# A hybrid attention layer on one core: a new opening, a row-wise end, and a forget chain laid around a softmax

## What is computed

```
n = rmsnorm(h); u = n @ w_in   # q, k, v of mixers A and B, 8 forget logits, 2 gates
A: chunk-band attention, 8 heads x 128, with a bias by distance
B: logits += F[t] - F[s], F = cumsum(log sigmoid(forget logit + b_f)), causal
h += (sigmoid(gate_A) * (o_A @ w_a) + sigmoid(gate_B) * (o_B @ w_b)) @ w_o
h += relu(rmsnorm(h) @ w_up)^2 @ w_down                 # 2048 -> 8192 -> 2048
h += (p @ w_ple_proj) * sigmoid(rmsnorm(h) @ w_ple_gate)
y = rmsnorm(h)
```

## Time and profile before

| | |
|---|---|
| median of 3 runs | 1919.04 us (1918.7 to 1919.19) |
| the profiled execution: its own time | 1919.11 us |
| its span in the trace | 1917.3 us |
| busy: PE | 1877.7 us, 98% of the span |
| busy: DVE, ACT, POOL | 902.6, 714.2, 210.4 us |
| DMA | 293.35 MB, 153 GB/s on average |

### The profile page before, as it was taken

One profiled execution on the slowest core, in us unless ns is written; L12 is line 12 of the kernel. 1 busy time (PEld: TensorE's weight loads), 2 busy tenths in 40 slices (PEclk: granted clock), 3 DMA queues, 4 the chain that ended last, 5 costly groups with the idle time before them and its releaser, 6 DMA issues.

```text
span 1917.3 us, 34966 instructions
## 1 busy us (share of the span) xinstructions
PE 1877.7 (98%) x12824; PEld 1873.2 (98%) x12824; DVE 902.6 (47%) x1113; ACT 714.2 (37%) x891; POOL 210.4 (11%) x287
## 2 busy tenths in 40 slices
PE   6999999999999999999999999999999999999996
PEld 5999999999999999999999999999999999999996
DVE  7444444444444444555444344443443444555455
ACT  5433333343333333333333333333333333333553
POOL 1111111110000000221000010000100001122123
PEclk9999999999999999999999999999999999999998
DMA  6544444445454444444444444444444444444442
GB/s 229 180 160 161 160 160 160 160 146 206 142 159 145 145 150 146 145 150 157 146 156 147 145 152 146 159 146 143 153 144 159 146 141 153 146 146 146 154 143 87
DMA packets 94146, 293.35 MB, mean 153 GB/s; under 512 B 13040, under 2 KB 26376, under 8 KB 93960
## 3 DMA queue, kind: packets, MB, share of 16 engines
q1 hardware_dynamic: 75312, 274.27, 43.8%
q10 hardware_dynamic: 18808, 18.72, 3.0%
HBM read 285.06 MB, written 9.46 MB: 154 GB/s over the span
## 4 chain that ended last, share of the span: by engine, by line
PE 96%; DVE 2%; issue 1%; ACT 0%; DMA 0%; DVEq 0%; POOL 0%; SPq 0%; POOLq 0%; ACTq 0%
PE banks L324 31%; PE banks L325 31%; PE banks L326 31%; DVE w_lo L773 1%; DVE x_lo L791 1%; PE banks L346 0%; PE banks L349 0%; PE banks L347 0%; DMA h<-in_x_t 0%; PE banks L474 0%; PE banks L475 0%; PE banks L476 0%; PE banks L375 0%; DVE rstd L785 0%; DVE h L248 0%
## 5 line engine op out<-in xcount | busy, mean ns | idle before, releaser
L500 ACT ACTIVATE w_hi<-w_raw 128x1024 fp32r<-128x1024 f32 x518 | 547.5, 1060 | 1019.4 <-PE banks L326 1007.8
L324 PE MATMUL banks<-x_hi,w_hi 128*128 128x320 f32 x2560 | 796.1, 311 | 2.6 <-DVE tmp L855 1.6
L326 PE MATMUL banks<-x_hi,w_lo 128*128 128x320 f32 x2560 | 791.1, 309 | 0.0
L325 PE MATMUL banks<-x_lo,w_hi 128*128 128x320 f32 x2560 | 790.9, 309 | 0.0
L773 DVE TENSOR_TENSOR w_lo<-w_raw,w_hi 128x1024 fp32r<-128x1024 f32 x518 | 615.5, 1223 | 32.5 <-ACT w_hi L500 32.5
L324 PEld LDWEIGHTS banks<-x_hi,w_hi 128*128 128x128 f32 x2560 | 480.7, 188 | 3.5 <-DVE tmp L855 1.8
L325 PEld LDWEIGHTS banks<-x_lo,w_hi 128*128 128x128 f32 x2560 | 480.8, 188 | 0.2
L326 PEld LDWEIGHTS banks<-x_hi,w_lo 128*128 128x128 f32 x2560 | 480.6, 188 | 0.0
L324 PE MATMUL banks<-o_hi,w_hi 128*128 128x320 f32 x1280 | 395.6, 309 | 0.0
L325 PE MATMUL banks<-o_lo,w_hi 128*128 128x320 f32 x1280 | 395.5, 309 | 0.0
L326 PE MATMUL banks<-o_hi,w_lo 128*128 128x320 f32 x1280 | 395.5, 309 | 0.0
(11 more groups left out here) (130 smaller groups left out, 956.6 us busy)
## 6 DMA issues: line engine op xcount, KB each, us to landing
w_raw<-in_w_slabs SPq DMA_DIRECT2D x518, 512.0 KB, 4.0
h<-in_x_t SPq DMA_DIRECT2D x4, 640.0 KB, 7.3
out_kv_t<-k_t ACTq DMA_DIRECT2D x16, 160.0 KB, 3.6
out_kv_t<-v_t ACTq DMA_DIRECT2D x16, 160.0 KB, 4.4
h<-in_x_t ACTq DMA_DIRECT2D x1, 2560.0 KB, 10.2
f_keys<-f_rows ACTq DMA_DIRECT2D x8, 224.0 KB, 3.2
out_y_t<-h ACTq DMA_DIRECT2D x2, 640.0 KB
bias_rows<-in_rel_rows ACTq DMA_DIRECT2D x1, 1024.0 KB
```

The source lines that it names most:

```text
L324: nc.tensor.matmul(out, w_hi[:, slot, ws], hi[:, xs], start=k == lo_k, stop=False)
L325: nc.tensor.matmul(out, w_hi[:, slot, ws], lo[:, xs], start=False, stop=False)
L326: mm = nc.tensor.matmul(out, w_lo[:, slot, ws], hi[:, xs], start=False, stop=k == hi_k)
L500: nc.scalar.activation(w_hi[:, slot, :], w_raw[:, slot, :], ACT.Copy).then_inc(s_whi, 1)
```

## The change: what it does

It joins three edits and a few smaller ones.

1. **Beginning.** The padded forget panel goes. Its 16 x 8 weights come in one 64 KB transfer, and lie in `wf`, high parts in columns 0 to 7 and the rest in columns 32 to 39 of each block, so that two matmuls a block give all products (L471, L472) and ACT and DVE add the two row groups. The q, k and v panels of the first unit are made half by half: feature blocks 0 to 7 for all three, then 8 to 15, in banks 2, 3 and 0. The input comes in five chunks, the first slab in two parts over ACT's queue. POOL's squares go to ACT; PE no longer waits for the forget sums to be read.
2. **Forget chain.** Its steps stand in three parts on DVE and two on ACT, between weight splits and around the softmax of the first unit. The unit that stood behind it is written out around it.
3. **End.** PE turns `h` into rows of tokens (12 pieces of up to 128 tokens x 512 features, six of them before the sums), the sums of squares are made as a column (one value a token), root and reciprocal are for 3 columns, and ACT and DVE scale the pieces while they copy them out of PSUM. SP stores them. The last gate block is done in two token halves.
4. **Smaller.** ACT's root takes the sum from PSUM with scale and bias (DVE's mean goes, at all norms); a table load for the root is moved ahead at `T_FF`; in the two `T_PLE` panels the bank groups change places, and PE's wait for the last read of `h` stands at the second slab; the gate panels use banks 4 and 5, and their token sum stands between the halves of the first one. There is one panel less, so every stage begins one panel number earlier.

```diff
-T_FORGET = 0
-T_UNIT = 1
+T_UNIT = 0
...
+HEAD = 3
+HEAD_SLABS = [2 * t for t in range(HEAD)] + [2 * t + 1 for t in range(HEAD)]
+HEAD_BANKS = (2, 3, 0)
+X_CHUNKS = ((0, 2), (2, 2), (4, 4), (8, 4), (12, 4))
...
+WF_STEP = 24
+WF_LOW = 32
+WF_COLS = WF_STEP * (KB - 1) + P
...
+Y_ROWS = ((0, 0, P), (P, 0, P), (TOK - P, P - (TOK - 2 * P), TOK - 2 * P))
+Y_BLOCKS = 4
+Y_PIECES = tuple((rows, group) for group in range(KB // Y_BLOCKS) for rows in range(len(Y_ROWS)))
+Y_BANKS = (0, 1, 2, 3, 7, 4 + T_GATE % 2, 4 + (T_GATE + KB - 1) % 2)
...
-            load_slab(w[0], 0)
-            load_x(0)
-            load_x(1)
+            for c in range(3):
+                load_x(c)
...
+            for n, (rows, group) in enumerate(Y_PIECES):
+                first, at, count = Y_ROWS[rows]
+                cols = slice(group * Y_BLOCKS * P, (group + 1) * Y_BLOCKS * P)
+                sp.wait_ge(s_scaled[n % 2], by_engine(n + 1, n % 2))
+                sp.dma_start(io["y"][first + P - count if at else first:first + P, cols], y_piece(n, False)).then_inc(s_stored, 16)
+            sp.wait_ge(s_stored, 16 * len(Y_PIECES))
...
+            def head_step(t, k, slot):
+                out = banks[:, HEAD_BANKS[t], 0:TOK]
+                ws, xs = slice(k % SLAB_KB * P, (k % SLAB_KB + 1) * P), slice(k * TOK, (k + 1) * TOK)
                 nc.tensor.matmul(out, w_hi[:, slot, ws], x_hi[:, xs], start=k == 0, stop=False)
                 nc.tensor.matmul(out, w_hi[:, slot, ws], x_lo[:, xs], start=False, stop=False)
-                mm = nc.tensor.matmul(out, w_lo[:, slot, ws], x_hi[:, xs], start=False, stop=k == KB - 1)
-                if kk == SLAB_KB - 1:
+                return nc.tensor.matmul(out, w_lo[:, slot, ws], x_hi[:, xs], start=False, stop=k == KB - 1)
+            def forget_step(k):
+                out, ws, xs = banks[:, FORGET, 0:TOK], slice(k * WF_STEP, k * WF_STEP + P), slice(k * TOK, (k + 1) * TOK)
+                nc.tensor.matmul(out, wf[:, ws], x_hi[:, xs], start=k == 0, stop=False)
+                nc.tensor.matmul(out, wf[:, ws], x_lo[:, xs], start=False, stop=k == KB - 1)
+            pe.wait_ge(s_wf_lo, 1)
+            for half in range(2):
+                for t in range(HEAD):
+                    s = half * HEAD + t
+                    for k in range(half * SLAB_KB, (half + 1) * SLAB_KB):
+                        if t == 0:
+                            pe.wait_ge(s_xlo, k + 1)
+                            forget_step(k)
+                        if s == 0 and k == 0:
+                            pe.wait_ge(s_first_lo, 1)
+                        elif k % SLAB_KB == (SLAB_KB // 2 if s == 0 else 0):
+                            pe.wait_ge(s_wlo, s + 1)
+                        mm = head_step(t, k, s % SLOTS)
                     mm.then_inc(s_mul, 1)
-            mix_in(Panel(T_UNIT), between=lambda: token_sums(0, 1))
-            mix_in(Panel(T_UNIT + 1), bank_read=True)
-            mix_in(Panel(T_UNIT + 2), bank_read=True)
+                    if s == HEAD + 1:
+                        pe.wait_ge(s_const, 3)
+                        token_sums(0, 1)
...
-            pe.wait_ge(s_acc, T_PLE)
             pe.wait_ge(s_mlo, KB + 2)
             for s in range(4):
                 pe.wait_ge(s_wlo, 2 * T_PLE + s + 1)
+                if s == 1:
+                    pe.wait_ge(s_acc, T_PLE)
                 after(pe, s_pread, s - 1)
                 for n in range(4):
-                    out = banks[:, 4 * (s % 2) + n, 0:TOK]
+                    out = banks[:, 4 * (1 - s % 2) + n, 0:TOK]
...
-            pe.wait_ge(s_pread, 4)
-            token_sums(2, 1 + 2 * KB)
-            gate(Panel(T_GATE))
+            def gate(t, between=None):
+                multiply(t, x_hi, x_lo, between=between, base=GATE_BANK)
+            pe.wait_ge(s_pread, 3)
+            gate(Panel(T_GATE), between=lambda: token_sums(2, 1 + 2 * KB))
...
+            def turn_piece(n):
+                rows, group = Y_PIECES[n]
+                first = Y_ROWS[rows][0]
+                for j in range(Y_BLOCKS):
+                    block = group * Y_BLOCKS + j
+                    src = h[:, block * TOK + first:block * TOK + first + P]
+                    tr = nc.tensor.transpose(banks[:, Y_BANKS[n % len(Y_BANKS)], j * P:(j + 1) * P], src, ident[:, :])
+                tr.then_inc(s_turned_y, 1)
+            ready_pieces = len(Y_BANKS) - 1
+            pe.wait_ge(s_hg, KB - 1)
+            for n in range(ready_pieces):
+                turn_piece(n)
...
-                act.wait_ge(s_mean, n)
-                nc.scalar.activation(mean[:, :], mean[:, :], ACT.Sqrt).then_inc(s_root, 1)
+                act.wait_ge(s_sum, n)
+                nc.scalar.activation(mean[:, :], banks[:, SUMS, 0:TOK], ACT.Sqrt, bias=eps[:, :], scale=1.0 / D_MODEL).then_inc(s_root, 1)
...
+            act.dma_start(wf_raw[:, :], io["w_forget"]).then_inc(s_wf, 16)
+            quarter_cols = SLAB // 2
+            act.dma_start(w_raw[:, 0, 0:quarter_cols], io["w_slabs"][0][:, 0:quarter_cols]).then_inc(s_first, 16)
+            act.dma_start(w_raw[:, 0, quarter_cols:SLAB], io["w_slabs"][0][:, quarter_cols:SLAB]).then_inc(s_slab[0], 16)
             act.dma_start(b_f[:, :], io["b_f"]).then_inc(s_forget, 16)
             act.dma_start(logf[:, 0:PAST], io["logf_cache_t"]).then_inc(s_forget, 16)
+            act.wait_ge(s_const, 3)
+            ready_root()
+            act.wait_ge(s_wf, 16)
+            act.wait_ge(s_zero, 2)
+            nc.scalar.activation(wf_part(0), wf_blocks, ACT.Copy).then_inc(s_wf_hi, 1)
             act.wait_ge(s_small, 16)
-            for n in range(KB):
-                if n % 4 == 0:
-                    act.wait_ge(s_x[n // 4], 16)
-                if n in (0, 6):
-                    split_weights(Panel(0), (n // 6,))
-                nc.scalar.activation(blk(x_hi, n), blk(h, n), ACT.Copy, scale=gain(MIX, n)).then_inc(s_xhi, 1)
-                if n in (11, 15):
-                    nc.scalar.activation(squares(n // 4), blk(h, n - 3, 4), ACT.Square).then_inc(s_sqa, 1)
+            for c, (first, blocks) in enumerate(X_CHUNKS):
+                act.wait_ge(s_x[c], 16)
+                for n in range(first, first + blocks):
+                    nc.scalar.activation(blk(x_hi, n), blk(h, n), ACT.Copy, scale=gain(MIX, n)).then_inc(s_xhi, 1)
+                if c == 0:
+                    act.wait_ge(s_first, 16)
+                    nc.scalar.activation(w_hi[:, 0, 0:quarter_cols], w_raw[:, 0, 0:quarter_cols], ACT.Copy).then_inc(s_first_hi, 1)
+                elif c == 1:
+                    act.wait_ge(s_slab[0], 16)
+                    nc.scalar.activation(w_hi[:, 0, quarter_cols:SLAB], w_raw[:, 0, quarter_cols:SLAB], ACT.Copy).then_inc(s_whi, 1)
+                elif c == 2:
+                    split_slab(1)
+                    split_slab(2)
+            split_slab(3)
...
+            split_weights(Panel(4), (0,))
             act.wait_ge(s_fdve, 3)
             nc.scalar.activation(tm(3)[0:HEADS], tm(2)[0:HEADS], ACT.Exp, scale=-1.0).then_inc(s_fact, 1)
+            split_weights(Panel(4), (1,))
+            split_weights(Panel(5))
+            store_kv(Unit(0, 0))
+            exps(Unit(0, 0))
             act.wait_ge(s_fdve, 4)
             nc.scalar.activation(tm(5)[0:HEADS], tm(4)[0:HEADS], ACT.Ln).then_inc(s_fact, 1)
-            split_weights(Panel(4))
+            split_weights(Panel(6))
...
             act.dma_start(tm(4, 2), io["p_t"]).then_inc(s_p, 16)
+            ready_root()
...
+            evacuate(Panel(T_UNIT), Unit(0, 0), 0, head_sum(0))
+            evacuate(Panel(T_UNIT + 1), Unit(0, 0), 1, head_sum(1))
+            split_weights(Panel(4), (0,))
+            evacuate(Panel(T_UNIT + 2), Unit(0, 0), 2, head_sum(2))
...
+            split_weights(Panel(4), (1,))
+            logits(Unit(0, 0))
+            evacuate(Panel(T_UNIT + 3), Unit(0, 1), 0)
+            split_weights(Panel(5), (0,))
+            invert(Unit(0, 0))
+            split_weights(Panel(5), (1,))
...
-            inverse_rms(4)
-            dve.wait_ge(s_hg, KB)
-            for first, blocks, by in Y_CHUNKS:
-                if by == 0:
-                    scale_output(nc.vector, first, blocks).then_inc(s_y[0], 1)
...
+            acc = summed(Panel(T_GATE + KB - 1), GATE_BANK)
+            n = KB - 1
+            for part in range(2):
+                nc.vector.tensor_tensor(token_half(tm(0), part), token_half(acc, part), token_half(rstd, part), ALU.mult).then_inc(s_gated[0], 1)
+            for part in range(2):
+                dve.wait_ge(s_gated[1], part + 1)
+                nc.vector.tensor_tensor(token_half(tm(2), part), token_half(tm(1), part), token_half(blk(ple_part, n), part), ALU.mult).then_inc(s_gated[2], 1)
+                dve.wait_ge(s_gated[2], part + 1)
+                nc.vector.tensor_tensor(token_half(blk(h, n), part), token_half(blk(h, n), part), token_half(tm(2), part), ALU.add).then_inc(s_plep, 1)
```

(20 more changed lines are left out.)

258 lines of the change are left out of this document (170 added, 88 removed).

## The result

| | before | after |
|---|---|---|
| median of the runs | 1918.87 us (1918.51 to 1919.19, 4 runs) | 1897.98 us (1897.21 to 1898.58, 4 runs) |
| ratio | | 0.9892 [0.9879, 0.9904] |
| profiled execution: own time, span | 1919.11, 1917.3 us | 1897.21, 1895.4 us |
| busy: PE, DVE, ACT, POOL | 1877.7, 902.6, 714.2, 210.4 us | 1881.0, 893.2, 725.8, 193.4 us |

The change makes the kernel 20.9 us faster by the medians (22.5 forecast), 21.9 by the two profiled executions. All three terms can be read from three points of PE: the first score matmul, the end E of the last panel, and the end of the span.

What follows compares the result with a forecast made beforehand. PE was taken to bound the kernel, busy 360.00 of 360 us mid-run; beginning 14.5, middle 3.9 and end 4.1 sum to 22.5 us off 1919.11, giving 1896.6 us, with 8 in 10 for 1891.5 to 1902.

Steps and rivals of the forecast that it cites:

- Beginning, 14.5: Up to PE's start of the first units' fourth panel: from 50.3 to 35.8 us, 14.5 us gained, bounds 11.5 to 17.
- The choice of the short DVE time: DVE's first slab at the start: taken at 1.21 us, not 3.23; if slow, the first full group comes 2 us later.
- The step of the clock: PE at the start: 4.4 us of slow running, 17 matmuls 0.26 apart until 12.15 us, then 0.147 apart.
- Cover at the fifth panel, 2.4 us: Second weight slab of the fifth panel, behind the forget chain: ready at 45.3, wanted by PE at 47.7 us.
- Middle, 3.9: PE's waits between beginning and end: removing them gains 3.1 + 3 x 0.26 = 3.9 us, bounds 2.5 and 4.2.
- All three waits: PE's waits for the second norm's slab (1.09), the last read of `h` (0.7), ACT's last `T_PLE` copy (1.3): gone.
- End, 4.1: From the last panel's matmul to the span's end: 19.06 us becomes 15.0, gaining 4.1, bounds 2 and 5.5.
- 2.62 MB take 6.85 + 1.7: Output stores at the end: moving at 0.383 MB/us takes 6.85 us, plus 1.7 of issue and latency.
- The rule about transposes: PE's end: a skill says transposes do not count as busy for the clock; if so, sums take 2 us more.
- No panel late: Rival in the beginning: a panel or two late through a slab or slow DVE, 2 to 6 us, chance 0.15.
- The slow first half: Clock rival: a 1.2 us hole keeps PE slow for 88 matmuls, 8 us more; chance 0.12 with the slow end.
- the change of even and odd panels: Rival at 255 panels' slab hand-over: swapped slots cost each a little; at 0.15 us a panel 1935 us, chance 0.04.

Runs made afterwards that it cites:

- e2_one_chain: The changed kernel with the forget chain in one piece on DVE and ACT, ahead of the first unit's softmax: 1901.90 us.
- e5_transposes: The changed kernel with 160 more transposes, whose result nobody reads, ahead of the output pieces: 1915.92 us, a single run.
- e3_pool_squares: The changed kernel with POOL squaring blocks 0 to 7 and adding four of them beside the opening, results unused: 1902.49 us.
- e6_prewarm: The changed kernel with 16 matmuls of ones into an unused bank ahead of everything on PE: 1896.29 us.
- e4_middle_undone: The changed kernel with the middle as before, but the mean still folded into the root: 1902.09 us, ratio to before 0.9913.
- e1_old_end: The changed kernel's opening and middle with the end of before (scaling of h in five chunks, transposed output): 1901.68 us.
- e8_prewarm_wide: The changed kernel with 16 warm-up matmuls of ones and six stores with 4 KB rows in place of twelve with 2 KB: 1895.55 us.
- e9_all_three: The changed kernel with warm-up matmuls, six wide stores, and 7 unread transposes in PE's idle 0.89 us at the end: 1896.13 us.
- e10_filled_gap: The changed kernel with only 7 extra unread transposes in PE's idle 0.89 us at its end: 1898.27 us.
- e0_after: The changed kernel timed again with no edit, where traces differ in when the clock steps up: 1898.58 us, ratio to before 0.9893.

## Why the prediction was right, point by point

- **What bounds the kernel**: right. The time follows PE's three points: in ten of the twelve traces with the new middle, whatever their ends do, 1836.8 us lie between the score matmul and E. The other two have waits of PE in between, `e2_one_chain` (1840.5) and `e5_transposes` (1837.6).
- **Beginning, 14.5; measured 14.58.** Input landing (5.4 forecast, ACT starts on it at 5.76), halves of slabs (0.6 and 0.7; 0.61 and 0.69) and the count of matmuls held. The choice of the short DVE time was right, and `e3_pool_squares` shows its reason. The step of the clock is the loose part, and the agreement to 0.1 us is luck. The prediction counted 4.4 us of slow running from the first full group; it was 3.4 in this trace (4.4 from PE's first matmul) and 2.3 to 5.2 in nine traces with this opening. With the score matmul at 42.28 to 43.87 in the three traces of the changed kernel the same term reads 13.5 to 15.1. `e6_prewarm` shows that the whole of the slow stretch is worth about 2 us.
- **Cover at the fifth panel, 2.4 us**: right. Ready at 45.30; `e2_one_chain` made PE wait there. Overlooked was the second wait, that of PE for POOL's softmax.
- **Middle, 3.9; measured 4.06**, 4.08 by `e4_middle_undone`. All three waits are gone, as forecast. One step of the working was wrong and did no harm: DVE's mean was counted as 0.5 us of the chain at `T_FF`, but it lay beside a weight split of ACT. What left the chain is 1.37 us, not 1.8, against a wait of 1.09, so 0.3 us was to spare and not 0.7.
- **End, 4.1; measured 3.3 in the trace and 3.1 by `e1_old_end`.** The term that was mis-sized is "2.62 MB take 6.85 + 1.7": at 318 GB/s they take 8.2 + 1.7, 1.4 more, of which the earlier first store gives back 0.7. The rate of 383 was right for the stores of 128 rows (372 to 387 with 2 KB rows). Wrong was to take it for all bytes: a fifth of them, the 64-row stores, move at some 197. As an estimate from these rows, 2.10 MB at 385 and 0.52 MB at 197 take 5.5 + 2.7 = 8.1 us, the 8.2 measured; with 4 KB rows at 405 it is 7.8, and `e8_prewarm_wide` has 7.83. So of the 1.4 us the row length is worth some 0.3 and the 64-row stores the rest. Wide stores made the end 0.6 shorter in two traces (15.2 for 15.8) and not at all in `e9_all_three` (15.9); that scatter is not explained. The same sum for before met its end partly by luck: its stores stood idle for part of the time, waiting for scaled chunks, and moved faster at a full share:

```profile
1909.00:1917.00 8.00, 0.00 (x0) 0.00 (x0) 5.27 (x2) 0.00 (x0) 4.26 (x2) 0.50 0.81 328
1913.00:1916.00 3.00, 0.00 (x0) 0.00 (x0) 1.27 (x1) 0.00 (x0) 0.26 (x1) 0.50 0.99 400
```

  The rule about transposes played no part; and where the clock fell no cost can be seen: E to the end is 15.8 in the first trace (20 transposes 4.06), 15.8 in `e10_filled_gap` (2.40) and 16.4 in `e0_after` (2.40).
- **Rivals.** No panel late (no wait of PE between 13 and 1879 us). The slow first half did not come. No loss by the change of even and odd panels: with the middle undone the score matmul is 1840.89 us ahead of E, to the hundredth what it was before.
- **Trace and median.** The forecast was made against profiled executions and missed the median by 1.4. The profiled execution of after was its fastest of four, for the reason in `e0_after`; 0.8 of the 1.4 is that, the rest the end, less the 0.2 that beginning and middle gained beyond the forecast.
